# Conformer output stage in another order, four high-part copies moved from ScalarE to VectorE

## The reference, cut to what matters

```python
proj = hm @ w_in + b_in
u_lru, gate_lru, conf_a, conf_b, bg_lru, bg_conf = jnp.split(proj, SPLITS, axis=-1)
xc, new_lru_buf = causal_dwconv(u_lru, lru_buf, lru_conv_w, lru_conv_b)      # width 4
hseq, h_last = rg_lru(xc, h0, start, lru_wa, lru_ba, lru_wx, lru_bx, lru_lambda)
out_a = (hseq * jax.nn.gelu(gate_lru)) @ w_lru_o
dc, new_conf_buf = causal_dwconv(conf_a * jax.nn.sigmoid(conf_b), ...)       # width 31
out_b = jax.nn.silu(layernorm(dc, conf_ln_g, conf_ln_b)) @ w_conf_o
merged = jax.nn.sigmoid(bg_lru) * out_a + jax.nn.sigmoid(bg_conf) * out_b
x = x + gt1 * (merged @ w_out)          # then the norm, the router and the experts
```

## Time and profile before

| what | value |
|---|---|
| median of three runs | 916.37 us |
| profiled execution | 926.14 us |
| its span, first to last instruction | 923.2 us |
| busy share of the span: PE, PEld, DVE, ACT, POOL | 93%, 79%, 75%, 49%, 32% |
| mean granted TensorE clock, share of full | 0.974 |
| chain that ended last, by engine | PE 37%, DVE 36%, DMA 14%, ACT 6% |

### The profile page before, as it was taken

How to read it: one execution, slowest core, us unless ns; L and a number is a source line. 1 busy time by engine, 2 the same in 40 slices (tenths; PEclk the granted TensorE clock), 3 DMA queues, 4 the chain that set the end, 5 groups by cost and what they waited for, 6 DMA issues and landing times.

```text
span 923.2 us, 13565 instructions
## 1 busy us (share of the span) xinstructions
PE 855.6 (93%) x5573; PEld 725.8 (79%) x5573; DVE 688.6 (75%) x961; ACT 452.3 (49%) x420; POOL 299.7 (32%) x179
## 2 busy tenths in 40 slices
PE   3899999998997998899999996899998999999996
PEld 2798888898996898899994456778876887777773
DVE  2529999999989897632023567789898989988967
ACT  5443232323269577441201033368767778776855
POOL 5344656745601000323310323103432334521105
PEclk9999999999999999999999996999999999999998
DMA  9978677422211212132446105589999999999962
GB/s 316 345 234 277 231 263 258 139 77 92 91 48 47 92 46 93 53 100 92 166 150 262 45 23 211 169 307 356 346 334 337 358 360 350 351 349 363 357 231 97
DMA packets 76395, 194.21 MB, mean 210 GB/s; under 512 B 7879, under 2 KB 48967, under 8 KB 65949
## 3 DMA queue, kind: packets, MB, share of 16 engines
q1 hardware_dynamic: 71245, 182.19, 55.6%
q0 software_dynamic: 4944, 10.78, 4.4%
q10 hardware_dynamic: 144, 0.38, 0.1%
HBM read 185.41 MB, written 15.95 MB: 218 GB/s over the span
## 4 chain that ended last, share of the span: by engine, by line
PE 37%; DVE 36%; DMA 14%; ACT 6%; issue 4%; SPq 1%; POOL 1%; DVEq 0%; ACTq 0%; POOLq 0%
PE ps L1327 21%; DVE ps L1736 13%; DVE slot_c L1944 8%; DMA ring_a<-in_w_up 8%; PE ps L1411 6%; DMA ring_a<-in_w_gate 4%; ACT slot_c L1105 3%; DVE slot_a L1944 2%; PE ps L1505 2%; PE ps L1287 1%; DMA region_c<-in_w_ada 1%; PE ps L1356 1%; SPq L544 1%; DMA ring_a<-in_w_down 1%; DVE region_b L2080 1%
## 5 line engine op out<-in xcount | busy, mean ns | idle before, releaser
L764 POOL TENSOR_TENSOR w_lo<-ring_a,w_hi 128x2048 fp32r<-128x2048 f32 x26 | 119.7, 4603 | 260.4 <-ACT w_hi L958 228.9
L1944 DVE TENSOR_TENSOR slot_c<-ring_a,slot_c 128x2048 fp32r<-128x2048 f32 x72 | 163.9, 2287 | 24.4 <-ACT slot_c L1105 23.8
L1105 ACT ACTIVATE slot_c<-ring_a 128x2048 fp32r<-128x2048 f32 x72 | 137.3, 1916 | 48.5 <-DMA ring_a<-in_w_gate 32.3
L1327 PE MATMUL ps<-hm_hi,w_hi 128*128 128x272 f32 x720 | 152.0, 292 | 8.8 <-ACT region_c L997 4.0
L1327 PE MATMUL ps<-hm_hi,w_lo 128*128 128x272 f32 x720 | 149.2, 290 | 0.0
L1327 PE MATMUL ps<-hm_lo,w_hi 128*128 128x272 f32 x720 | 148.9, 289 | 0.0
L1736 DVE SCALAR_TENSOR_TENSOR ps<-region_b,rt,ps 128x512 f32<-128x512 f32 x208 | 137.6, 743 | 0.0
L1327 PEld LDWEIGHTS ps<-hm_hi,w_hi 128*128 128x128 f32 x720 | 113.1, 190 | 23.7 <-issue 22.9
L1505 PE MATMUL ps<-slot_c,xgt_hi 128*128 128x512 f32 x384 | 127.2, 401 | 3.1 <-DVE slot_c L1944 1.8
L1327 PEld LDWEIGHTS ps<-hm_lo,w_hi 128*128 128x128 f32 x720 | 113.7, 190 | 0.0
L1327 PEld LDWEIGHTS ps<-hm_hi,w_lo 128*128 128x128 f32 x720 | 113.2, 190 | 0.0
(11 more groups left out here) (354 smaller groups left out, 1506.9 us busy)
## 6 DMA issues: line engine op xcount, KB each, us to landing
ring_a<-in_w_gate SPq DMA_DIRECT2D x32, 1024.0 KB, 8.0
ring_a<-in_w_up SPq DMA_DIRECT2D x32, 1024.0 KB, 8.2
ring_a<-in_w_down SPq DMA_DIRECT2D x32, 1024.0 KB, 7.2
ring_a<-in_w_in SPq DMA_DIRECT2D x24, 1024.0 KB, 6.9
region_c<-in_w_ada SPq DMA_DIRECT2D x20, 1024.0 KB, 5.7
ring_a<-in_w_conf_o SPq DMA_DIRECT2D x4, 1024.0 KB, 5.1
ring_a<-in_w_lru_o SPq DMA_DIRECT2D x4, 1024.0 KB, 5.3
region_d<-in_w_ada SPq DMA_DIRECT2D x3, 1024.0 KB, 12.8
```

What stands on the lines that cost most here:

```text
L764: g.tensor_tensor(w_lo[:, q % 2], raw[split_at[q] % 2], w_hi[:, q % 2].bitcast(F32), ALU.subtract)\
L1105: s_.activation(hi_slot(n), raw_slot(n), ACT.Copy).then_inc(unit_hi, 1)
L1327: ins = mm(ps[:, bank(n) + h, 0:HALF], w[:, q % 2, k, m * P:(m + 1) * P], x[:, k, h * HALF:(h + 1) * HALF], start=(k == 0 and w is w_hi an ...
L1944: v.tensor_tensor(lo_slot(n), raw_slot(n), hi_slot(n).bitcast(F32), ALU.subtract).then_inc(unit_lo, 1)
```

## The change

It alters the order of the stage and moves four copies:

- `work`: the group r2 i2 r3 i3 moves from behind co0.3 to behind BD0, r4 i4 r5 i5 from behind BD2 to behind BD3, and r6 i6 r7 i7 from behind co1.0 to behind co1.2.
- ACT: the loop over the normalised blocks keeps the Silu of all eight, and the copy to the high part of the first four only. DVE copies the high parts of blocks 4 to 7 itself, each just ahead of the subtraction.
- ACT: where a piece's last use is an "in" chunk with a gate group right behind it, the high part of the piece that follows is made behind that group's read-out (this holds for piece 23, which goes behind i5). The waits of an r item stand ahead of the wait for its product. The high part of z is made behind BL0 and not behind BL1.
- DVE: the convolution steps of blocks 2 and 3 move out of the loop over blocks, the scan gets a step of its own (`lru_scan`), and the "co" read-outs, the low parts of the pieces and the recurrent steps stand in another order. DVE makes the low parts of pieces 24, 25 and 26 too, which POOL made; POOL begins with piece 27. `last_rows(1, ...)` (line 1823) goes behind the low part of z and piece 26.
- SP: pieces 26 and 27 are loaded ahead of the stores of the last rows, not behind them.

```diff
-                if (h, w, m) == (1, "co", 2):
-                    work += [(x, 1, c) for c in range(2) for x in ("r", "i")]
+                if (h, w) == (1, "co") and m in (0, GC - 1):
+                    k0 = 2 if m == 0 else GC
+                    work += [(x, k // GC, k % GC) for k in (k0, k0 + 1) for x in ("r", "i")]
             for m in range(GC):
                 work += [(w, h, m)]
-                if (h, w, m) in ((0, "co", GC - 1), (1, "co", 0)):
+                if (h, w, m) == (1, "co", 2):
                     work += [(x, h, c) for c in range(2, GC) for x in ("r", "i")]
...
         for q in range(2, len(split_at)):
-            split_after.setdefault(last_use(split_at[q - 2]), []).append(q)
+            at = last_use(split_at[q - 2])
+            if work[at + 1][0] == "r" and work[at][0] == "in":
+                at += 4
+            split_after.setdefault(at, []).append(q)
...
-            rows_at = piece_of[("in", G_BL, 1)] + 1
+            rows_at = piece_of[("lo", 0, 1)] + 1
...
-            pool.wait_ge(w_lo_ok, 24)
-            for q in range(24, len(split_at)):
+            pool.wait_ge(w_lo_ok, 27)
+            for q in range(27, len(split_at)):
                 split_lo(q)
...
+                if kind == "r":
+                    act.wait_ge(last_tr, 1)
+                    if (g * GC + m) % 2 == 0 and g + m:
+                        act.wait_ge(z_ok, (g * GC + m) // 2)
                 act.wait_ge(pairs, n + 1)
...
-                    for k in range(KC + 1):
...
-                        if k:
+                    for k in range(KC):
+                        act.wait_ge(ln_ok, k + 1)
+                        s_.activation(dc[:, k, :], dc[:, k, :], ACT.Silu, ...).then_inc(sn_ok, 1)
+                        if 0 < k <= GC:
                             act.wait_ge(sn_ok, k)
                             s_.activation(dc_hi[:, k - 1, :], dc[:, k - 1, :], ACT.Copy).then_inc(dc_hi_ok, 1)
...
-                if (kind, g, m) == ("in", G_BL, 1):
+                if (kind, g, m) == ("in", G_BL, 0):
...
             for k in range(KC):
+                if k >= GC:
+                    dve.wait_ge(sn_ok, k + 1)
+                    dve.wait_ge(dc_hi_ok, k)
+                    v.tensor_copy(dc_hi[:, k, :], dc[:, k, :]).then_inc(dc_hi_ok, 1)
                 dve.wait_ge(dc_hi_ok, k + 1)
                 v.tensor_tensor(dc_lo[:, k, :], dc[:, k, :], dc_hi[:, k, :].bitcast(F32), ALU.subtract)\
                  .then_inc(dc_lo_ok, 1)
-                if k % 4:
-                    lru_tap(2 + k // 4, k % 4)
-                else:
-                    lru_bias(2 + k // 4)
+                if k in (0, 2):
+                    lru_bias(2 + k // 2)
+            lru_tap(2, 1)
+            lru_tap(2, 2)
+            lru_tap(2, 3)
```

More of the change, by code:

```diff
@@ L1008, in drain @@
                     k = g * GC + m
-                    act.wait_ge(last_tr, 1)
-                    if k % 2 == 0 and k:
-                        act.wait_ge(z_ok, k // 2)
                     ins = s_.activation(two(tt[:, m % 2, :]), pair(n), ACT.Sigmoid, bias=rt[:, k, R_BA:R_BA + 1])
@@ L1070, in _ @@
                 if (kind, g, m) == ("in", G_BC, 3):
-                    for k in range(KC + 1):
[L1073 to L1076, removed]
-                        if k:
+                    for k in range(KC):
+                        act.wait_ge(ln_ok, k + 1)
+                        s_.activation(dc[:, k, :], dc[:, k, :], ACT.Silu, bias=rt[:, k, R_LNB:R_LNB + 1],
+                                      scale=rt[:, k, R_LNG:R_LNG + 1]).then_inc(sn_ok, 1)
+                        if 0 < k <= GC:
                             act.wait_ge(sn_ok, k)
@@ L1804, in lru_3, with lru_scan @@
                 ch.do(v.memset(first_step(xp), 0.0))
-                ch.link(v.memset(xp[:, :, 0:1], 0.0))
+                ch.do(v.memset(xp[:, :, 0:1], 0.0))
+            def lru_scan(p):
+                ch.wait()
                 ch.link(v.tensor_tensor_scan(rec_flat, xc_flat[p % 2], ii_flat, 0.0, ALU.mult, ALU.add))
@@ L1884, in gated @@
                     v.tensor_tensor(merged[:, k, :], merged[:, k, :], bg[m], ALU.add).then_inc(merged_ok, 1)
+            gated("co", 0, 0)
             w_low(19)
             lru_1(0)
-            gated("co", 0, 0)
+            lru_tap(3, 1)
             lru_2(0)
+            lru_tap(3, 2)
+            lru_tap(3, 3)
             gated("co", 0, 1)
@@ L1892, in _ @@
             gated("co", 0, 2)
+            w_low(20)
+            lru_scan(0)
             lru_4(0)
-            w_low(20)
             gated("co", 0, 3)
@@ L1897, in _ @@
             lru_conv(4)
+            lru_conv(5)
             lru_1(1)
-            lru_conv(5)
+            w_low(21)
             lru_2(1)
-            w_low(21)
             lru_3(1)
+            lru_scan(1)
             lru_4(1)
+            w_low(22)
             dve.wait_ge(z_ok, 2)
@@ L1907, in _ @@
             lru_1(2)
+            w_low(23)
+            gated("co", 1, 0)
             lru_2(2)
-            w_low(22)
             lru_3(2)
+            lru_scan(2)
+            gated("co", 1, 1)
             lru_4(2)
-            gated("co", 1, 0)
-            w_low(23)
+            w_low(24)
+            gated("co", 1, 2)
             lru_1(3)
             lru_2(3)
-            gated("co", 1, 1)
+            gated("co", 1, 3)
             lru_3(3)
+            lru_scan(3)
             lru_4(3)
+            w_low(25)
             dve.wait_ge(z_ok, 4)
-            last_rows(1, 35, 1)
-            gated("co", 1, 2)
-            gated("co", 1, 3)
             for h in range(2):
@@ L1927, in _ @@
                 v.tensor_tensor(z_lo[:, hs], z[:, hs], z_hi[:, hs].bitcast(F32), ALU.subtract).then_inc(z_lo_ok, 1)
+            w_low(26)
+            last_rows(1, 35, 1)
             for h in range(2):
```

## The result

Over 13 runs each the changed kernel took 911.13 us (median, 908.43 to 916.62) and the kernel before 920.9 us (916.3 to 925.99): a ratio of 0.9894, 95% interval 0.9867 to 0.9922. Faster, as forecast; but 911.13 is 6.6 us above the predicted 904.5 and 0.13 us above the end of the range. Of the 6.6 us, 4.5 are the base, which stands at 920.9 and not at 916.37; the other 2.1 are the difference of the medians, 9.8 us for 11.9, and the interval (7.2 to 12.2 us of 920.9) holds both.

A forecast was written before the change was run, and what follows sets the result against it. TensorE's split-precision products at line 1327 were taken to set the stage's pace, other engines counting only through its waits. 1.9 + 2.1 + 4.1 + 4.5 - 0.7 = 11.9 us, so 916.37 becomes 904.5 us; range 901 to 911.

The forecast's parts named there:

- a full queue: VectorE's queue, first chunk to co1.2: 3 us late plus one halved clock, gain 7.2, 909.2 us; 2 us beyond gives 911.
- First chunk: co0.0: VectorE copies blocks 4 to 7, convolution steps leave the loop, last subtraction starts earlier; gain 1.9 us.
- r2 to i3: Gate group moved behind BD0, where ScalarE's high part and table load pass during TensorE's chunk; gain 2.1 us.
- Before co1.0: Low part of piece 22 made earlier ends TensorE's wait: 2.41 plus 1.7 for the clock, gain 4.1 us.
- before BL0: co1.2's read-out put ahead of the last pair's scan ends TensorE's wait: 2.81 plus 1.7 for the clock, 4.5 us.
- The wait at i6: Added TensorE wait, as i6 needs co1.2's banks and its read-out comes at T + 19.8 against T + 19.0; cost 0.7 us.
- the r items' waits in another order: ScalarE's changed order of waits at r items: an edit at no price that takes away no work.
- the first rival: VectorE becomes the bound, tightest at w_low(20), which BD0 needs: 19.4 us of queue against 19.5; 909.2 us, chance 0.17.
- The low parts on VectorE: Pieces 24 to 26, 2.28 us each on VectorE replacing GpSimd's 4.63: listed among the edits at no price.
- scan was stretched: Rival: three scans on VectorE's filled queue each 4.24 us longer; 4.2 us slower, 920.6 us, chance 0.04.
- absorbed: Rival: the experts, fed by transfers, swallow the gain after the stage; 916.4 us would stay, chance 0.07.

The follow-up runs named there:

- experiment 1: Both kernels run again unaltered: the kernel before against itself 1.0014, the changed kernel 0.9873 against the kernel before, 912.5 us.
- experiment 6: Changed kernel with ScalarE copying all eight high parts, co1.2's read-out ahead of piece 24's low part, r items waiting for their product first: 0.9807, 907.59 us.
- experiment 3: Kernel before with useless small matmuls filling TensorE's waits before r3, co1.0 and BL0: 0.9959 to the kernel before, stage 197.26 us.
- experiment 4: Changed kernel with the low parts of pieces 24 to 26 back on GpSimd: 0.9886 to the kernel before, stage 190.55 us.

## Why the prediction was right in the stage and wrong in the total

**The step that failed** is the last one of the sum: "It stands 9.8 us above the median; I have no reason to put that difference into this stage, so the median becomes 916.37 - 11.9 = 904.5 us." That the 9.8 us are not in this stage still seems fair: the stage of the kernel before took 199.73 us in the execution of 926.14. What was wrong is the base. The median of three runs, 916.37, lay at the bottom of this kernel's spread: in later rounds its medians were 923.58 (20 runs), 925.13 (9), 924.39 (11) and 925.26 (12). The profiled execution was nearer to the ordinary and the three runs were low ones; 926.14 beside 916.3 to 919.98 was the sign of it, and I set it aside. Why the first runs were low, by chance or by something that differed between the rounds, is not shown. With 920.9 the same 11.9 gives 909.0, and as a ratio it is 1 - 11.9 / 916.37 = 0.987, inside the measured interval.

**The range** failed in the same step. Its high end was built from this stage alone (a full queue, 2 us beyond), with nothing for a base that can itself lie off, by 4.5 us here and by 7 to 9 in the later rounds. The spread of about 10 us between runs of one kernel is as large as the effect.

**Where the spread sits** is only in part shown. The tail, the same code in both, took 430.7 to 440.8 us in the profiled executions here, 434.7 to 440.8 in those with the old order and 430.7 to 440.3 in those with the new. In it the experts' weights stream in: from 590 to 850 us at 352 GB/s in the shortest tail, at 341 GB/s in a long one (windows, the last column):

```profile
590.00:850.00 260.00, 255.94 (x1222) 206.12 (x1221) 234.83 (x254) 192.22 (x136) 80.78 (x26) 1.00 0.97 352
```

```profile
590.00:850.00 260.00, 250.73 (x1186) 199.72 (x1185) 228.04 (x248) 187.33 (x132) 81.78 (x26) 1.00 0.96 341
```

The first is the changed kernel in experiment 1, the second the version of experiment 6. Whether the slower transfers make the tail long or only go with it, and what sets their rate from one execution to the next, was not tried and stays open, as does whether the new order shortens the tail by a little on average.

**The terms.** *First chunk*, 1.9 predicted: 2.2. From the first subtraction to the last it was 10.32 us and is 8.10. The mis-sized part is the copy, 0.43 to 0.44 us where I took 0.54 from line 1753, the row of an operation with two per-partition operands (why that one is slower was not tried); with 0.44 the same sum gives 2.3. *r2 to i3*, 2.1: 2.1 (16 matmuls in 3.98; a table load at 317.28 us stands ahead of BD0's sigmoid, and none ahead of r2's). *Before co1.0*, 4.1, and *before BL0*, 4.5: both whole, against the execution that the rows are from; that the 1.7 us in each are the clock's was read from one window in co1.0 (0.50 in 354 to 356), and with the waits filled 3.0 of the 3.4 came back (experiment 3). *The wait at i6*, -0.7: -1.2, as the group takes 369.96 - 364.77 = 5.19 us for 3.98. 0.88 us of it stand before i6, for the read-out named; the rest stands before r7, for r6's sigmoid behind the table load. My own terms here add up to T + 19.9, not 19.8, so the forecast should have been -0.9; 0.88 is close to that, and the table load was missing. That the r items' waits in another order take away no work was true and beside the point: they moved the load behind the product, for 0.74 us with what the same order cost at the two other groups. Actual terms: 2.2 + 2.1 + 4.1 + 4.5 - 1.2 = 11.7. Two smaller slips changed nothing: the queue of the first rival adds up to 19.25 us, not 19.4, and ScalarE's last Silu stood behind six copies, not seven.

**What was luck.** "So a wait of 2.4 us or more cost 1.7 us on top" was read from one execution, and the runs don't bear it out as a fixed price: in three executions of the old order the wait before r3 (2.08 or 2.09 us) cost 0, 1.6 and 1.7 us, and the wait before BL0 (2.79 to 2.81) 1.6, 1.6 and nothing. Against the second execution of the kernel before the stage gained 13.1 us and not 11.7. That the sum came within 0.2 us of one pair of executions is thus partly luck, as is that the first chunk's 0.3 more than forecast made up for part of the 0.5 more that the wait at i6 cost.

**What was costed at nothing.** The low parts on VectorE are worth 2.5 us (experiment 4). My sum held that gain without naming it, inside the wait before BL0 and inside a wait at i6 with scans of 2.42.

**The rivals.** VectorE did not become the bound: no wait of TensorE on line 1843 (before: 1836), and behind the first chunk, with its three of 0.39 to 0.61 us, the only waits in the stage are those in the group r6 to i7 and, as before, the 1.78 us ahead of line 1414. No scan was stretched; what stretches was met in experiment 4. The gain was not absorbed: the tail did not grow. BL0 and line 1414 came at 376 and 474.68 us (predicted 376 and 474.6).

## What to carry to other kernels

Predict a ratio, or a difference against the execution whose rows were read, and take the base's own spread into the range; a profiled execution 1% above the few timed runs is a sign that they do not show the spread. When a reordering carries a name, price its parts apart: here the named part cost 1 to 2 us, and the steps that moved with it paid for that and for the rest. And where two delays lie side by side, take both away before concluding that one of them is free.

## What the runs showed of the hardware

- Small VectorE instructions that met a GpSimd split were held until its end: in experiment 4 a copy of 66 columns took 3.75 us for 0.2, an addition of 16 columns 4.63 for 0.19, as in the kernel before the scan 6.66 for 2.42. A read-out (0.72 us at 360.84 in experiment 4) ran at full speed beside the split from 360.12; one of its two inputs comes from PSUM. The three that were held read no PSUM. Why they were held and the read-out was not, no run shows.
- Waits of about the same length cost the clock in some executions only: behind 2.09 us before r3 it stayed at 1.00, behind 2.08 us it fell to 0.50 twice; behind 2.79 and 2.81 us before BL0 it fell to 0.50, behind 2.80 us it stayed at 1.00. The wait of 1.78 us ahead of the experts was followed by 16 matmuls in 8.80 us in two executions of the kernel before, and in 7.11 us in three of the changed one; with the copies alone or the filled waits, in the old order, it was 7.10, so it is not the order that decides.
- With several waits ahead of an activation that needs a table load, their order in the code decided which of them the load carried: 0.44 us in the one group with such a load, of 0.74 us that the order of the waits cost in the stage.
